# Two PEER layers on one core: row numbers of the gathered tile ahead of the dense tiles', a new table of early steps

## What is computed

```
q = (xb @ w_q).reshape(128, 8, 2, 128)               # 8 heads, two halves
s = einsum('thpd,hpnd->thpn', q, sub_keys)            # 128 scores for each half
s_top, i_top = top_k(s, 16)
cand = s_top[..., 0, :, None] + s_top[..., 1, None, :]
best, pos = top_k(cand.reshape(.., 256), 16)          # 16 of 256 pairs
expert = (i_top0 * 128 + i_top1) at pos               # 128 experts a token
g = softmax(best)
act = gelu(einsum('td,thkd->thk', xb, u[expert]))
out = einsum('thk,thkd->td', g * act, v[expert])      # u, v: 16384 x 1024
```

## Time and profile before

| what | value |
|---|---|
| median of 3 runs | 3347.74 us |
| the profiled execution, its time | 3350.17 us |
| its span in the trace | 3348.4 us |
| PE busy | 3096.9 us, 92% |
| DVE busy | 2462.3 us, 74% |
| ACT busy | 1311.1 us, 39% |
| POOL busy | 1342.1 us, 40% |
| mean granted TensorE clock | 0.961 |
| HBM read | 921.87 MB |

### The profile page before, as it was taken

How to read it: one execution, slowest core, us unless ns; L and a number is a source line. 1 busy time by engine, 2 the same in 40 slices (tenths; PEclk the granted TensorE clock), 3 DMA queues, 4 the chain that set the end, 5 groups by cost and what they waited for, 6 DMA issues and landing times. The chain is left out here.

```text
span 3348.4 us, 46062 instructions
## 1 busy us (share of the span) xinstructions
PE 3096.9 (92%) x16440; PEld 2061.0 (62%) x16440; DVE 2462.3 (74%) x5627; ACT 1311.1 (39%) x3317; POOL 1342.1 (40%) x1040
## 2 busy tenths in 40 slices
PE   7999899789999998989699999997899999999887
PEld 2466488656666666655344554786666666666553
DVE  5874369979799788877721253599888898788777
ACT  3232122476556555500101162224675565555100
POOL 0000000536566677767300000005356567667765
PEclk9999999899999999999899989998899999999999
DMA  8510262869999999999812101527789999999998
GB/s 293 186 51 26 95 226 70 302 221 391 387 372 400 409 398 409 409 409 409 340 56 82 59 11 38 201 70 269 249 341 392 368 399 408 396 409 409 409 409 346
DMA packets 282683, 931.23 MB, mean 278 GB/s; under 512 B 31804, under 2 KB 32460, under 8 KB 281944
## 3 DMA queue, kind: packets, MB, share of 16 engines
q0 software_dynamic: 147840, 536.96, 41.1%
q1 hardware_dynamic: 134616, 391.34, 31.1%
HBM read 921.87 MB, written 6.32 MB: 277 GB/s over the span
## 5 line engine op out<-in xcount | busy, mean ns | idle before, releaser
L739 PE MATMUL psum<-hT,mod 128*128 128x256 f32 x4096 | 983.0, 395 | 56.5 <-ACT big L1197 52.7
L739 PEld LDWEIGHTS psum<-hT,mod 128*128 128x128 f32 x4096 | 791.7, 198 | 182.4 <-issue 76.1
L1207 ACT ACTIVATE levels<-key_numbers,hT 128x128 bf16<-128x128 f32 x1712 | 541.7, 388 | 318.2 <-PE psum L775 318.2
L1860 DVE SCALAR_TENSOR_TENSOR tmp<-w,small,tmp 128x1024 f32<-128x1024 f32 x339 | 435.8, 1285 | 68.1 <-DMA w<-in_peer_up,tmp 32.9
L2035 POOL DMA_INDIRECT w<-in_peer_u,tmp x172 | 237.3, 1380 | 595.0 <-DVEq L1688 457.8
L1840 DVE CUSTOM_DVE_ANT_0 w<-w,hn 128x1024 f32<-128x1024 f32 x342 | 408.8, 1224 | 70.2 <-DMA w<-in_peer_u,tmp 36.6
L2035 POOL DMA_INDIRECT big<-in_peer_down,tmp x86 | 116.1, 1350 | 722.3 <-DVEq L1688 645.2
L749 PE MATMUL psum<-rows,big 128*128 128x512 f32 x768 | 345.4, 593 | 4.1 <-DVE big L1793 4.1
L775 PEld LDWEIGHTS psum<-x,levels 128*128 128x128 bf16 x6144 | 226.7, 101 | 187.6 <-issue 133.2
L775 PE MATMUL psum<-x,levels 128*128 128x32 bf16 x6144 | 238.3, 196 | 70.3 <-issue 30.8
L1223 ACT ACTIVATE small<-small 128x4 f32<-128x4 f32 x128 | 26.3, 205 | 641.3 <-DVE small L1840 641.2
(11 more groups left out here) (324 smaller groups left out, 4278.7 us busy)
## 6 DMA issues: line engine op xcount, KB each, us to landing
mod<-in_uT SPq DMA_DIRECT2D x256, 512.0 KB, 6.8
rows<-in_peer_v SPq DMA_DIRECT2D x64, 512.0 KB, 6.8
rows<-in_peer_up SPq DMA_DIRECT2D x64, 512.0 KB, 6.8
w<-in_w_in SPq DMA_DIRECT2D x14, 2048.0 KB, 8.3
srow<-in_peer_v SPq DMA_DIRECT2D x32, 512.0 KB
tmp<-in_peer_v SPq DMA_DIRECT2D x32, 512.0 KB
srow<-in_peer_up SPq DMA_DIRECT2D x32, 512.0 KB
tmp<-in_peer_up SPq DMA_DIRECT2D x32, 512.0 KB
```

What stands on the lines that cost most here:

```text
L739: last = nc.tensor.matmul(ps[4 + e % 2][:, 0:ND], ub[e % UV][:, k, :], hT[:, k, ND:SEQ], start=k == 0, stop=k == KC - 1)
L1207: last = nc.scalar.activation(hits[n % HITS][:, j * P:(j + 1) * P], keyno, ACT.Abs, bias=nibT[:, n * BATCH + j:n * BATCH + j + 1])
L1860: last = stt(y, row, c8[g % 2][:, b:b + 1], y, ALU.mult, ALU.add)
```

## The change

It puts the row numbers of gathered tile 0 ahead of the last numbers and the softmax of the dense tiles on DVE (with two more buffers for numbers); gives PE and ACT 9 + 3 blocks in place of 3 + 5 around the turning of the dense numbers; lets 12 instead of 8 blocks be done ahead of the key phase; lowers the number of batches in the first eight steps; and starts the choice of tile 1 at step 8.

```
 def batches_due(e):
-    return 0 if e < 0 else min(LATER, 2 * e + 4 + min(4, e // 2))
+    short = EARLY - AHEAD
+    if e < short:
+        return 0 if e < 0 else 4 + e
+    return min(LATER, 2 * e + 8, 4 + short + (e - short + 1) * 13 // 5)
 def copies_due(e):
-    return 0 if e < 0 else min(LATER // 4, (e + 1) // 2 + 1)
+    return 0 if e < 0 else min(LATER // 4, (e + 1) // 2 + 1, batches_due(e + 1) // 4)
 def blocks_before(n):
-    return 8 + (EARLY - 8) * n // BATCHES
+    return 12 + (EARLY - 12) * n // BATCHES
 def pieces_due(e):
-    return min(PIECES, (e + 1) * 5 // 6)
+    return max(0, min(PIECES, e + 1 - (EARLY - AHEAD)))
...
+        ia.append(gate[:, SLOTS:2 * SLOTS])
+        ib.append(part(tmp, 4.5, 0.5))
+        of_tile = {0: 2, 1: 0, 2: 0, 3: 1}
...
             def first_experts(layer):
-                for e in range(3):
+                for e in range(9):
                     first_product(layer, e)
                 for n in range(len(DENSE)):
                     turn_picks(layer, n)
-                for e in range(3, 8):
+                for e in range(9, 12):
                     first_product(layer, e)
...
             def first_acts(layer):
                 for e in range(3):
                     block_gelu(layer, e)
+                gate_exp(0)
+                for e in range(3, 9):
+                    block_gelu(layer, e)
                 for n in range(len(DENSE)):
                     copy_picks(layer, n)
-                block_gelu(layer, 3)
-                gate_exp(0)
-                for e in range(4, 8):
+                for e in range(9, 12):
                     block_gelu(layer, e)
...
             def peer(layer):
                     for t in DENSE:
                         at_once(head_experts(t, p))
-                    if p == 2:
-                        for t in DENSE:
-                            at_once(numbers(t, 0, EARLY_HEADS))
                 for t in DENSE:
                     start_gates(t)
-                    at_once(numbers(t, EARLY_HEADS, NH))
-                for p in range(3):
+                for p, t in enumerate((2, 3, 0)):
                     dve.wait_ge(sc_used, 32 * layer + 16 + 4 * (p + 1))
                     at_once(head_experts(0, p))
-                for t in DENSE:
-                    finish_gates(t)
+                    at_once(numbers(t, 0, EARLY_HEADS))
                 dve.wait_ge(sc_used, 32 * (layer + 1))
                 at_once(head_experts(0, 3))
                 start_gates(0)
-                dve.wait_ge(picks_turned, len(DENSE) * (layer + 1))
-                at_once(numbers(0, 0, EARLY_HEADS))
                 at_once(numbers(0, EARLY_HEADS, NH))
                 expert_rows(0)
+                for t in DENSE:
+                    at_once(numbers(t, EARLY_HEADS, NH))
+                for t in DENSE:
+                    finish_gates(t)
                 finish_gates(0)
```

More of the change, by code:

```diff
@@ L1667, in numbers @@
                         step(tt(oh[:, 0:k * slots], oh[:, 0:k * slots], oh[:, k * slots:2 * k * slots], ALU.add))
-                    step(tt(dst[t % 2 if t in DENSE else 0][:, c], oh[:, 0:slots], oh[:, slots:2 * slots], ALU.add))
+                    step(tt(dst[of_tile[t]][:, c], oh[:, 0:slots], oh[:, slots:2 * slots], ALU.add))
                     yield
@@ L1685, in expert_rows @@
                 step = picks
-                step(stt(idf, ia[0], float(NKEY), ib[0], ALU.mult, ALU.add))
+                step(stt(idf, ia[of_tile[t]], float(NKEY), ib[of_tile[t]], ALU.mult, ALU.add))
                 step(nc.vector.tensor_copy(idx[:, t * SLOTS:(t + 1) * SLOTS], idf))
```

## The result

The changed kernel takes 3390.65 us, the median of 4 runs (3389.87 to 3392.61), against 3349.69 (3345.48 to 3353.01, 4 runs) for the kernel before: ratio 1.012, 95% interval 1.0106 to 1.0134. It is 41 us slower; the forecast was 24. The time lies 3 us above the range that was given for the forecast itself (3356 to 3388), and inside the wide range (3341 to 3393), which had been stretched to take in the third rival. The profiled executions say the same: a span of 3389.6 us against 3348.4, +41.2.

A forecast was written before the change was run, and what follows sets the result against it. PE's clockwork was taken to set step 61, where the DMA tail starts. Terms of 6.2 - 7.0 + 3.8 + 9.2 = 12.2 us a layer, 24.4 for two, gave 3372 us; own range 3356 to 3388, wide range 3341 to 3393.

The forecast's parts named there:

- the third rival: Gaps on PE behind early gate copies: the clock falls in each, 21.8 us a layer, 3391 us; chance 0.11.
- A: Start of the steps: late dense numbers delay batch 0 and DVE's first unit by 8.1 us; +6.2 us a layer.
- D: Eight steps from 8 to 19: gate copies wait for PE's next batches, holding back a gelu PE needs; +9.2 a layer.
- B: Steps 0 to 7: fewer batches make steps 1 to 7 shorter, 29.2 instead of 36.2 us; -7.0 us a layer.
- Bound: Steps up to 61: PE's clockwork sets step 61's time, the DMA tail starts there; DVE bounds the key phase.
- DVE's wait in step 61: Wait for quarter 2's last gate copy: to end near 1182 instead of 1169.47 us, its length above 12.
- There PE gets 1.9 back: End of the key phase: product 22 no longer stands between batches 59 and 60, so PE regains 1.9 us.
- C: Steps 8 to 23: ten batches moved out of the early steps come where PE is full; +3.8 us a layer.
- No stall (1): Gate copies on ACT: no stall behind them, 3.0 us a layer, 3354 us; chance 0.22.
- the transfers (2): From step 8 on: transfers, not PE, decide; a layer gains 5.9 us, 3336 us, faster; chance 0.11.

The follow-up runs named there:

- e9: Kernel before with 12 instead of 8 blocks ahead of the key phase (3 + 9), DVE's order as it was: 3360.67 us, ratio 1.0023.
- e5: Changed kernel with gate copies never ahead of their batches and 9 instead of 12 blocks ahead of the key phase: 3361.7 us, ratio 0.9996.
- e10: Kernel before with DVE's new order alone, blocks 3 + 5 as before: 3384.45 us, ratio 1.0092.
- e4: Kernel before with the change's tables of batches, copies and pieces, but gate copies never ahead of their batches: 3351.47 us, ratio 0.9994.
- e11: Kernel before with no batch in step 0, two in each of steps 1 to 7, gate copies never ahead, later choice: 3338.35 us, ratio 0.9956.
- e1: Changed kernel with gate copies due only when PE's batches of the same step have made their group: 3373.55 us, ratio 1.0065.
- e2: Kernel before with the change's tables of batches, copies and pieces alone, start of the stage as it was: 3372.99 us, ratio 1.0058.
- e6: Kernel before with the later choice of the second gathered tile alone, from step 8 on: 3365.44 us, ratio 1.0006.

## Why the prediction was right, and where it was wrong

The sign, the mechanism and the places were right; the sum was 24.4 us where the traces show 41.2, so it was short by 17: about 7 in A, 6 in D, 1 in B, and 2.5 outside the terms. Term by term, for layer 0 / layer 1:

- **Bound.** Right. The column "rest" shows it in fourteen kernels. One sign that I named was wrong: DVE's wait in step 61 did not grow above 12 us but fell to 9.38 and 6.33. DVE's first keys now wait for PE's batches (44.4 us between 755 and 1169, all at L1774; before 15.5, at L1770), so DVE has less lead. That cost nothing, as PE still came last.
- **A, start: forecast +6.2, measured +8.3 / +11.5.** The order of events came as written: behind the first product, `top_ready` 23.2 us (forecast 23.4), batch 0 52.4 (53.6), the first unit 54.2 (55.6), so 6.7 us late instead of 8.1; PE turns the first dense tile before the second is done, which I had not counted. The step that failed is the last one, "There PE gets 1.9 back". From DVE's last spread to the start it lost 1.8 in layer 0 (6.25 to 8.06) and 2.9 in layer 1 (8.59 to 11.44). I saw that a product no longer stood between batches 59 and 60, and booked it as time won; it was the cover of batch 63's spread on ACT, and PE stands for 1.69 and 1.70 instead. The rest of layer 1 is the clock: two products there take 5.38 and 5.39 us, where before one takes 6.04. e9 shows this part alone, e5 and e10 the other: the blocks between late numbers and batch 0. In layer 1 the first unit is 8.4 late, as the three products behind the turning took 13.07 us instead of 11.22, with a granted clock of 0.81 instead of 0.94.
- **B: forecast -7.0, measured -7.4 / -5.5.** Right. B and C together in e4: -2.8 / -1.6, forecast -3.2. Its lower bound of -9.2 was wrong: it left all 21 batches in, although C adds the ten moved ones again. With 11 the sum is 44.6 less 8 x 3.43 and 11 x 0.38, 13.0, and e11's steps 0 to 7, with 14, gain 11.3.
- **D: forecast +9.2, measured +11.1 / +12.9 (after against e1).** The eight steps, the releaser and the lengths were right: a gap shows as 1.44, 1.06 to 1.10 or 0.70 to 0.74, to which the 0.16 of a product's overhang belongs, and 1.60, 1.22 and 0.84 were forecast for none, one and two batches left. Together 9.6. The rest is the clock, which I took not to fall: it fell behind one of the two longest gaps in layer 0 and behind both in layer 1, 5.38 - 3.69 = 1.7 us each. The bound I had kept for it took 1.2 for a fall, which is too little, and a fall behind every gap, which is too much: the other thirteen left it alone. By the rule of the Trainium skill ("TensorE: Matmul & The Clock Gate", Part 1, on oscillation) that I had set against the rows, brief idleness can make the clock swing; the trace agrees for 3 gaps of 16 only.
- **Rivals.** No stall (1) and the transfers (2) are out, by the eight gaps and by the column "rest". The third, 3391, hit the time to the microsecond and is wrong all the same: it had a fall of the clock in all sixteen gaps and A at 6.2. Its surplus stands where A's shortfall and some scatter were. The hit is luck: sixteen falls at the measured 1.7 would have been 3399.
- **The range.** It was said to have A and B at their ends. These give 3.1 and 17.1 us a layer, so 3354 to 3382 on the median, not 3356 to 3388; the measured 3391 is outside both. A passed its upper bound of 8.1 in both layers, and a fall of the clock had no room between these ends.
- **What is left, about 4 us,** lies behind step 61 in layer 0 (+2.1) and in the mixer of block 2 (+2.1), which the change doesn't touch. From the first dense tile's sum to layer 1's first product the profile of before has 600.4 us, the kernel after 602.5, and the others 602.6 to 605.2, the ones that time like before among them. So nothing ties it to this change. Whether it is scatter or comes with any edit isn't shown, as there is one profile of before; what makes it stays open.
- **The idea of the change,** rows sooner, gave nothing: 13.5 us of lead on the same scale ended in six full buffers.

## What to carry to other kernels

A wait that is moved one step ahead in an in-order queue costs what stands behind it: ask which engine wants the next entry, and when. Work that keeps an engine busy between two waits isn't always in the way; before counting its removal as a gain, see which slower engine refills a buffer under it. And the early steps were worth thinning, but the gain lay in the rate (two batches a step, below what ACT can spread) and not in the number moved: the change's own table gave 2 us, no more than the noise, the even one 14.

## What was not expected of the hardware

A gap of one and the same length sometimes lowers the clock and sometimes doesn't. In the kernel after, gaps shown as 1.44 us left the next product at 3.69 us once and at 5.38 three times; in e2, at 5.38 twice in layer 0 and at 3.69 twice in layer 1. That is five of eight. None of the 24 gaps of 0.70 to 1.11 us in the two kernels slowed the product behind it.

The other thing is the second group of runs, with the kernel before included 9 to 14 us slower than the others. In its profiles PE stops several times near 631 us inside a batch with nothing to wait for ("issue" in the trace, 2.4 us in e6's key phase against 1.2 before), and DVE then waits for that batch. Stops of this name are not a mark of the group alone: the kernel after has 3.5 us of them, without a wait of DVE behind them. What makes them, and whether they account for the group, stays open. That is why kernels were compared within a group.
